# A fused transformer layer on one core: the first modulation in column quarters instead of halves, with the first projection's chunks between them

## What is computed

```python
mod = (silu(c) @ w_ada + b_ada)
shift1, scale1, gate1, shift2, scale2, gate2 = split(mod, 6)
h = rms_norm(x, norm1_w) * (1.0 + scale1) + shift1
proj = h @ w_in                      # q, k, v of dilated attention; four parts of HGRN2
```

## Time and profile before

| | us |
|---|---|
| runs of the kernel before | 2439.27, 2435.23, 2437.67 (median 2437.67) |
| time of the profiled execution | 2437.41 |
| its span | 2435.4 |
| PE busy | 2357.8 (97% of the span) |
| DVE busy | 1594.3 (65%) |
| ACT busy | 1036.1 (43%) |

### The profile page before, as it was taken

How to read it: one execution, slowest core, us unless ns; L and a number is a source line. 1 busy time by engine, 2 the same in 40 slices (tenths; PEclk the granted TensorE clock), 3 DMA queues, 4 the chain that set the end, 5 groups by cost and what they waited for, 6 DMA issues and landing times.

```text
span 2435.4 us, 27909 instructions
## 1 busy us (share of the span) xinstructions
PE 2357.8 (97%) x10954; PEld 1966.4 (81%) x10954; DVE 1594.3 (65%) x1282; ACT 1036.1 (43%) x874; POOL 47.8 (2%) x55
## 2 busy tenths in 40 slices
PE   4899999998999999999999999999999999999999
PEld 3777888887888888888887888878888888888887
DVE  7878989986666666655568456556565555555554
ACT  2255553435343333333334556664443433433432
POOL 1011000000000000000000000000000000000000
PEclk9789999999999999999999999999999999999999
DMA  9988997654676776655655545535555555555553
GB/s 353 377 296 316 355 320 263 248 204 156 224 239 223 242 242 227 217 185 185 190 179 170 187 156 163 164 129 165 178 191 187 189 187 190 189 189 189 189 189 104
DMA packets 235129, 520.30 MB, mean 214 GB/s; under 512 B 9705, under 2 KB 10162, under 8 KB 232370
## 3 DMA queue, kind: packets, MB, share of 16 engines
q1 hardware_dynamic: 234352, 519.15, 63.1%
q10 hardware_dynamic: 706, 0.17, 0.0%
HBM read 517.19 MB, written 2.10 MB: 213 GB/s over the span
## 4 chain that ended last, share of the span: by engine, by line
PE 90%; DVE 4%; DMA 2%; ACT 2%; issue 1%; DVEq 1%; POOL 1%; ACTq 0%; SPq 0%
PE PS L257 28%; PE PS L259 27%; PE PS L258 27%; DMA ada_raw<-in_w_ada_dram 2%; PE PS L1626 2%; PE PS L1665 1%; PE PS L1600 1%; DVE w_lo L247 1%; PE PS L306 1%; ACT w_hi L243 1%; PE PS L1610 1%; POOL rstd L570 1%; DVE ada_acc L1097 0%; DVE MS L1042 0%; DVEq L1448 0%
## 5 line engine op out<-in xcount | busy, mean ns | idle before, releaser
L247 DVE TENSOR_TENSOR w_lo<-raw,w_hi 128x2048 fp32r<-128x2048 f32 x392 | 897.5, 2291 | 697.3 <-ACT w_hi L243 692.3
L243 ACT ACTIVATE w_hi<-raw 128x2048 fp32r<-128x2048 f32 x392 | 751.0, 1916 | 1154.9 <-PE PS L259 1143.3
L257 PE MATMUL PS<-w_hi,A_hi 128*128 128x512 f32 x2112 | 838.3, 397 | 8.5 <-DVE A_lo L361 4.0
L259 PE MATMUL PS<-w_hi,A_lo 128*128 128x512 f32 x2112 | 826.9, 392 | 0.0
L258 PE MATMUL PS<-w_lo,A_hi 128*128 128x512 f32 x2112 | 826.4, 391 | 0.0
L257 PEld LDWEIGHTS PS<-w_hi,A_hi 128*128 128x128 f32 x2112 | 399.9, 189 | 90.6 <-issue 2.9
L259 PEld LDWEIGHTS PS<-w_hi,A_lo 128*128 128x128 f32 x2112 | 399.0, 189 | 84.6
L258 PEld LDWEIGHTS PS<-w_lo,A_hi 128*128 128x128 f32 x2112 | 399.8, 189 | 81.1 <-issue 1.0
L257 PE MATMUL PS<-w_hi,H_hi 128*128 128x512 f32 x1024 | 401.6, 392 | 1.5 <-issue 1.3
L259 PE MATMUL PS<-w_hi,H_lo 128*128 128x512 f32 x1024 | 398.9, 390 | 0.0
L258 PE MATMUL PS<-w_lo,H_hi 128*128 128x512 f32 x1024 | 398.5, 389 | 0.0
(11 more groups left out here) (265 smaller groups left out, 1107.0 us busy)
## 6 DMA issues: line engine op xcount, KB each, us to landing
raw<-in_w_ff_dram SPq DMA_DIRECT2D x128, 1024.0 KB, 5.2
raw<-in_mlp_w_in_dram SPq DMA_DIRECT2D x64, 1024.0 KB, 5.3
raw<-in_mlp_w_out_dram SPq DMA_DIRECT2D x64, 1024.0 KB, 5.0
raw<-in_w_in_dram SPq DMA_DIRECT2D x56, 1024.0 KB, 8.1
X<-in_w_ada_dram SPq DMA_DIRECT2D x96, 512.0 KB, 5.8
raw<-in_sb_w_qkv_dram SPq DMA_DIRECT2D x48, 1024.0 KB, 5.1
ada_raw<-in_w_ada_dram SPq DMA_DIRECT2D x32, 1024.0 KB, 10.0
raw<-in_w_out_dram SPq DMA_DIRECT2D x16, 1024.0 KB, 6.6
```

What stands on the lines that cost most here:

```text
L243: act.activation(w_hi[:, j, :, :], raw[:, j, :, :], ACT.Copy).then_inc(hi_rdy, 1)
L247: dve.tensor_tensor(w_lo[:, j, :, :], raw[:, j, :, :], w_hi[:, j, :, :].bitcast(F32), ALU.subtract).then_inc(lo_rdy, 1)
L257: pe.matmul(bank(pair + t), h, w_hi[:, j, k, :], start=first, stop=False)
L259: mm = pe.matmul(bank(pair + t), l, w_hi[:, j, k, :], start=False, stop=last)
```

## The change

- The first shift and scale are done in four quarters of 512 shift and 512 scale columns. A piece is 128x1024 (512 KB), 16 per quarter and 64 in all, in a ring of eight.
- PE takes pieces 1, 3, 5, 7, 9, 11 and 13 of the first quarter; DVE takes the other nine, and all 16 of each further quarter.
- `quarter_sums`, `quarter_modulation` and two steps of turning follow each quarter. Chunks 3q to 3q+2 stand on PE after quarter q for q = 0, 1, 2, so nine chunks come before the last quarter's steps and three after. The order of the 12 chunks is q, k, v for each quarter of the contraction, so q is complete after chunk 9, k after chunk 10 and v after chunk 11.
- x is loaded after four pieces of 512 KB instead of four of 1 MB. The masks at the head of DVE's program move behind pieces 0 and 2, `first_root` behind piece 4, `level_masks` into the second quarter and `bounds_and_angles` into the third. The low parts of chunks 0 to 9 are made between pieces (`LOW_AFTER`).
- The first group's q and k are squared, normalised and turned at slots 10 to 13 instead of 8 to 12, through bank 6, and its attention runs one slot later (`STAGE_LAG`). Chunk 12 waits for q's normalisation instead of for the copy of q turned.
- The other modulation's pieces start at slot 10 instead of 7, and slots 17, 21, 36, 37, 49 and 50 have three instead of two. The collections come to stand in slots 17, 24, 32, 39, 50 and 61.

```diff
-AT0_ORDER = [(b, k) for h in range(2) for b in range(3) for k in (2 * h, 2 * h + 1)]
-HEAD = CH * 3 // 2
-ADA_BY_PE = (3, 7, 11), (7, 11)
+QUARTERS = D // NC_
+RING = 2 * CH
+AT0_ORDER = [(b, k) for k in range(QUARTERS) for b in range(3)]
+HEAD = 3 * (QUARTERS - 1)
+ADA_BY_PE = (1, 3, 5, 7, 9, 11, 13), (), (), ()
+STAGE_LAG = 1
...
+LOADS_AFTER = {(0, 8): 0, (1, 0): 1, (1, 3): 2, (1, 8): 3, (2, 0): 4, (2, 4): 5, (2, 9): 6, (3, 0): 7, (3, 4): 8, (3, 9): 9}
+LOW_AFTER = {(0, 12): 0, (1, 5): 1, (1, 8): 2, (1, 13): 3, (2, 4): 4, (2, 8): 5, (2, 13): 6, (3, 4): 7, (3, 8): 8, (3, 13): 9}
...
+ADA_FROM = HEAD + 1
+ADA_NONE = range(CH * OUT0 - 1, CH * OUT0 + 2)
+ADA_ONE = tuple(range(CH * (OUT0 - 4), CH * (OUT0 - 4) + 7)) + (CH * OUT0 + 3,)
+ADA_THREE = 17, 21, 36, 37, 49, 50
...
+            for q in range(QUARTERS):
+                turn_act(act, 0, g1, mod[:, SHIFT1, :], turned, steps=(2 * q, 2 * q + 1), first=2 * q, banks=QUARTER_BANKS)
+                for n in range(3 * q + 1, 3 * q + 4):
+                    split_hi(act, n // CH, n % CH)
...
+            def quarter_modulation(q):
...
+                dve.wait_ge(ada_pe, ada_share(q, KT - 1, True))
+                dve.wait_ge(ada_sum, q + 1)
+                dve.tensor_reduce(sums, bank(QUARTER_BANKS[1], 0, 8 * n).rearrange("p (c m) -> p c m", m=n), AX_X, ALU.add)
...
+            for q in range(QUARTERS):
                 for k in range(KT):
...
+                    if (q, k) == (0, 0):
+                        counts()
+                    if (q, k) == (0, 2):
+                        masks()
+                    if (q, k) == (0, 4):
+                        first_root()
+                    if q and k == 0:
+                        quarter_modulation(q - 1)
+                    if q and k in (1, 2):
+                        turn_first(2 * (q - 1) + k - 1)
+                    if (q, k) == (1, 7):
                         level_masks()
-                        first_root()
-                    if (h, k) == (0, 9):
+                    if (q, k) == (2, 5):
                         dve.wait_ge(rstd_rdy, 1)
                         bounds_and_angles()
...
+            for q in range(QUARTERS):
+                pe.wait_ge(y_rdy, q + 1)
+                turn(0, X, steps=(2 * q,), first=2 * q, banks=QUARTER_BANKS[:1])
+                quarter_sums(q)
+                pe.wait_ge(mod_rdy, q + 1)
+                turn(0, X, steps=(2 * q + 1,), first=2 * q + 1, banks=QUARTER_BANKS[1:])
+                if q < QUARTERS - 1:
+                    for n in range(3 * q, 3 * q + 3):
+                        at0_chunk(pe, n)
...
-                        if s % CH == 0:
+                        if i == 1 and s == 0:
+                            pe.wait_ge(n_mul, 1)
+                            used[p] += 1
+                        elif s % CH == 0:
                             take(p)
...
-        return {"square": (8, 10), "norm": (9, 11), "turn": (10, 12), "copy": (11, 12)}
+        return {"square": (10, 11), "norm": (11, 12), "turn": (12, 13), "copy": (13, 13)}
```

More of the change, by code:

```diff
@@ L350, in turn_act, with turn_dve @@
                     between[pos]()
-        def turn_dve(dve, n, g, s=None, tmp=None, steps=ALL, first=0, banks=WIDE, between=None):
+        def turn_dve(dve, n, g, s=None, tmp=None, steps=ALL, first=0, banks=WIDE, between=None, tmp_at=0):
             dve.drain()
@@ L754, in _ @@
                 normalise(act, X, X, c)
[L755 to L762, removed]
+            split_hi(act, 0, 0)
+            for q in range(QUARTERS):
+                turn_act(act, 0, g1, mod[:, SHIFT1, :], turned, steps=(2 * q, 2 * q + 1), first=2 * q, banks=QUARTER_BANKS)
+                for n in range(3 * q + 1, 3 * q + 4):
+                    split_hi(act, n // CH, n % CH)
             groups = proj_groups()
@@ L956, in _, with counts, masks @@
             d()
+            def counts():
+                for mask, dst in ((3, f_a), (15, f_b)):
+                    dve.tensor_scalar(tmp_i, dist, mask, None, ALU.bitwise_and)
+                    d()
+                    dve.tensor_scalar(dst, tmp_i, 0.0, None, ALU.is_equal)
+                    d()
+                dve.scalar_tensor_tensor(out=f_a, in0=dist, scalar=float(S + P), in1=f_a, op0=ALU.is_le, op1=ALU.add)
+                d()
+                dve.tensor_tensor(f_a, f_a, f_b, ALU.add)
+                d()
+                dve.scalar_tensor_tensor(out=count[:, :], in0=dist, scalar=float(S), in1=f_a, op0=ALU.is_ge, op1=ALU.mult)
+                d()
+            def masks():
+                dve.tensor_scalar(maskadd[:, :], count[:, :], 0.5, None, ALU.is_gt)
+                d()
+                dve.tensor_scalar(maskadd[:, :], maskadd[:, :], -NEG, NEG, ALU.mult, ALU.add)
+                for c in (2, 3):
+                    dve.tensor_scalar(f_b, count[:, :], float(c), float(np.log(c)), ALU.is_equal, ALU.mult)
+                    d()
+                    dve.tensor_tensor(maskadd[:, :], maskadd[:, :], f_b, ALU.add)
+                    d()
+                dve.tensor_scalar(neg_s[:, :], above[:, :], -NEG, NEG, ALU.mult, ALU.add)
             def level_masks():
+                low = setup[:, 0:P]
                 dve.tensor_tensor(xor_i, rows_i, cols_i, ALU.bitwise_xor)
@@ L1028, in step_modulation, with turn_first @@
                                          op0=ALU.add, op1=ALU.mult).then_inc(g_rdy, 1)
-            def turn_first(steps, first, **more):
-                turn_dve(dve, 0, g1, mod[:, SHIFT1, :], turned, steps=steps, first=first, **more)
-            for h in range(2):
+            def turn_first(step):
+                turn_dve(dve, 0, g1, mod[:, SHIFT1, :], turned, steps=(step,), first=step,
+                         banks=QUARTER_BANKS[step % 2:step % 2 + 1], tmp_at=step % 2)
+            for q in range(QUARTERS):
```

214 lines of the change are left out of this document (81 added, 133 removed).

## The result

The changed kernel takes 2446.93 us, the median of 7 runs (2445.28 to 2447.85), against 2438.97 for the kernel before, also 7 runs (2435.23 to 2440.76). The ratio is 1.0030, interval 1.0020 to 1.0039: slower, by 8.0 us. The forecast was 2446.7, which is 9.0 above the 2437.67 that it started from. The profiled execution lasted 2447.66 us with a span of 2445.7, 10.3 more than the one before; the median moved 8.0, so some 2 us of what follows belong to these two executions (the one before lay 1.6 under its median, this one 0.7 over).

A forecast was written before the change was run, and what follows sets the result against it. The start was taken as bound by 33.5 MB of pieces and DVE's adding, later groups by PE with DVE close behind. Chunk 12 +3.0, +7 after slot 19, slot 26 +2: +9 on 2437.4, plus 0.26, gave 2446.7 us; range 2433 to 2453.

The forecast's parts named there:

- The landings and the first quarter: Start: piece 4 lands at 20.55, PE's pieces end at 39.8, the quarter's sums are complete on DVE at 42.3.
- The turnovers: After each complete quarter: 16 sum records at half clock, 3.6 us; DVE gets its next piece 9.25 us later, losing nearly 5.6.
- Chunk 9 and the clock: After the last quarter: chunk 9 starts at 157.3, pays 2.0 us for half clock and ends at 164.75.
- its first 12 matmuls: Chunk 9's slow part, taken from chunk 0: 5.3 us where full clock needs half of 5.45, so 0 to 2.6 lost.
- The first attention: Slots 15 to 26: PE loses 1.3 us in slot 15, waits 8 in slot 19; stalls anything from 0 to 12.
- +7 in the sum: Lateness after slot 19's wait: +5.8 us, made +7 by half clock and one more step of the lagged attention.
- rival 3: HGRN2 groups: DVE's lag carries on, extra pieces in slots 36, 37, 49 and 50 all show; +5, 2452; 8%.
- the slot 26 term: Next attention's first maximum, slot 26: collections in slot 24 instead of 22 make PE wait, +2 us.
- 1, full clock: Quarters: sums and restarts run at full clock, each turnover 1.75 us shorter, chunk 9 without slow part; 2431; 15%.
- 2, stalls do not grow: First attention: DVE absorbs the collections, so only the +3 us at chunk 12 stays; 2440.7; 22%.
- 4, halved transfers fall short: Quarters: 512 KB transfers below 0.35 MB per us outlast DVE's 33.25 us; at 0.30, 2463; 5%.

The follow-up runs named there:

- e2_fill: On the changed kernel, the modulation of quarters 1 to 3 follows the third piece of the next quarter instead of the first; 2440.68 us, ratio 1.0002.
- e5_warm: On the changed kernel, 16 discarded 128x512 products on PE ahead of the sums of quarters 2, 3 and 4; 2441.86 us, ratio 1.0010.
- e1_defer: On the changed kernel, the two collections of slot 17 moved to slot 22; 2449.57 us, ratio 1.0042.
- e4_late: On the changed kernel, the third pieces of slots 17 and 21 moved to slots 28 and 30; 2446.47 us, ratio 1.0029.
- e6_fill_warm: On the changed kernel, e2_fill with 20, 20 and 10 discarded products ahead of the sums and e7_zero's zero products; 2435.33 us, ratio 0.9984.
- e3_pe2: On the changed kernel, PE instead of DVE takes pieces 11 and 14 of each further quarter; 2444.47 us, ratio 1.0021.
- e7_zero: On the changed kernel, 14 products of a zero tile on PE ahead of chunk 9; 2445.15 us, ratio 1.0021.

## Why the prediction was right, and where it was not

**How much of the hit is luck.** The forecast was +9.0 on a kernel before of 2437.67, and +8.0 on 2438.97 was measured. That the two times lie 0.2 us apart is chance; a step of 9 for 8 is what was forecast well, and some of its terms were off in both directions.

**The landings and the first quarter.** DVE takes up piece 4 at 22.67, where its landing was put at 20.55. It makes chunk 0's low part at 38.2 for 37.4; then come the sums at 43.1 for 42.3 and chunk 0 at 52.3 for 51. PE's pieces end at 42.0, not 39.8; the transposes follow, and the quarter's sums begin at the end of PE's work as much as at the end of DVE's. The mask work at the head cost nothing, as said: DVE waits 3.17 us right behind it.

**The turnovers.** DVE's wait for the sums (2.94 to 3.25 for the 2.8 worked out), the 16 records of 3.6 us and chunks 3 and 6 came as forecast. PE idled 5.0 us ahead of the third sums, where "some 5 us" was said. In e2_fill PE still idles 5.0 us there, and the time falls all the same: what this edit wins back is DVE's wait for the sums, while PE's idle time ahead of them costs by the half clock that follows it (e5_warm).

**Chunk 9 and the clock.** The last quarter was 1.1 faster than the sum had it (sums at 147.56 for 148.65), and chunk 9 began at 155.6 for 157.3. But its slow part cost 3.3 us (8.7 for 5.45), not the 2.0 taken and more than the bound of 2.6: the step "its first 12 matmuls" is undersized, since in chunk 9 the half clock lasts 14 products. The two errors nearly cancel: chunk 9 ended at 164.4 for 164.75. Chunk 12 then went without the wait for q, as forecast, since q's normalisation was done in time, and started at 175.0 for 175.65.

**The first attention.** Slot 15's wait was 1.21 for 1.3. Slot 19's was 5.47 for 8: PE came there at 226.7, not 225.4, and the transposes started at 232.1, not 233.4. Slot 26 took 0.4 of the 2 allotted. K's turn of slot 24 is 7.2 later than before (259.85 to 252.69), +7 in the sum. What failed is the reason given for it. The text put the loss on the two collections of slot 17; with them moved (e1_defer) the time did not fall. What the traces bear out is the wider statement behind it: from chunk 13 to chunk 33 DVE has 4.5 us more to do than before, at 89% busy, and PE gets what it waits for later by about as much. That this work is the cause is argued, not shown: no run took work out of the stretch. Two other orders of DVE's work were tried there (e1_defer, e4_late); both moved the waits between the slots and neither avoided the loss. Whether an order exists that does stays open, and so does what DVE's own waits for ACT's normalised q and k add.

**After slot 26** the sum had nothing more (+9 in all at slot 26, with 2 of them there). Measured: 8.3 at low part 33, 9.2 at 63, with a wait for `kT`. So the end was right with a piece of rival 3 in place of the slot 26 term, which is luck.

**Rivals.** *1, full clock:* did not happen in this kernel, and its price is real. e5_warm got 5 us from it, and e6_fill_warm, with the wait filled too, came to 2435, where 2431 was worked out. In the first quarter PE works on pieces for 10.4 us without a break from 31.62 to 42.0, at 0.217 per record, and the sums at 43.09 take 3.57: still half clock. The Trainium skill (TensorE: Matmul & The Clock Gate, Part 1) has half rate as the default that activity lifts; by that alone those sums would have taken 1.8, and the row disagrees: 3.57, behind 10.4 us of one-column products and four transposes without a break. *2, stalls do not grow:* fell, 2.84 became 5.47, and e6_fill_warm shows the loss with a start 10.7 us earlier. *3, lag carries on:* about 1 us of its 5. *4, halved transfers fall short:* fell; in quarters 2 to 4 DVE never waited for a piece in the changed kernel, and DMA moved 407 GB/s at 110 to 120. The Trainium skill (DMA: Bandwidth & Descriptors, Bandwidth) advises transfers of at least 1 MiB; going against it cost nothing here, with up to eight of 512 KB queued.

## What to carry to other kernels

Cutting a reduction into more parts lets the consumer start earlier, but each part has a turnaround of its own: before starting, ask what the bound engine does during it, and put work of the next part there (e2_fill: 6.3 us). Work brought forward only helps if the next place that sets the pace is relieved too; here a lead of 7.6 us shrank to 1.9 in the first stretch in which DVE is nearly as full as PE. And where PE stands still for some us ahead of short products, a few products of zeros in the gap can be worth more than a new order of the work, if they end before the real one is ready.

## What the runs showed of the hardware that was not expected

- **Runs of one-column products went by without the clock rising, and with it falling.** 48 of them in 10.40 us without a break (31.62) left the sums behind them at half rate. In e3_pe2, begun at full clock behind a chunk, 32 of them went by at 0.12 each, and then four transposes and 16 more at half rate (0.21 each), with no idle time between. The kernel before pays for this too: behind its pieces at 97.09 the first seven products of chunk 3 stand 0.43 apart, although PE has not idled. Behind 5.59 us of 128x128 products of zeros, chunk 9 ran at full clock (e7_zero).
- **The clock column is empty at the start.** The next rows are windows of the kernel after. They show a granted clock of 1.00 while every one-column record takes 0.22 us, nearly twice what it takes behind a chunk:

```profile
20.00:30.00 10.00, 6.09 (x30) 6.08 (x29) 7.21 (x8) 0.00 (x0) 1.29 (x1) 1.00 1.05 407
30.00:40.00 10.00, 9.28 (x45) 9.20 (x44) 5.51 (x4) 6.81 (x9) 1.35 (x1) 1.00 1.05 406
```

  The first clock record of this trace stands at 56.0 us, where chunk 0's products go from 0.43 to 0.23 apart, and the column counts time without a record as full clock. So before it the 1.00 says nothing, and the records' pace, half, is what there is to go by. In the kernel before the first clock record stands at 59.6, so its 0.65 at 60 to 70 can be used.
- **Partly fast sums.** After 1.36 us of idle time 16 records took 2.76 us, between 1.95 and 3.57 (e5_warm): the granted clock is 1.00 from 79.82 to 80.70 and 0.50 from 80.80 to 82.58, so it fell in the middle of them.
